# Dilated attention by residue class, with a joint softmax from exchanged maxima and sums

## What is computed

```python
for g, (window, dilation) in enumerate(DILATED_GROUPS):
    o_g, l_g = dilated_window_attention(q[:, :, g], k, v, window, dilation)
    outs.append(o_g)
    lses.append(l_g)
wts = jax.nn.softmax(jnp.stack(lses, axis=0), axis=0)
o = jnp.einsum('gbsh,gbshd->bshd', wts, jnp.stack(outs, axis=0))
y = o.reshape(Bsz, S, B_VW) * jax.nn.silu(z.astype(jnp.float32))
return y.astype(h.dtype) @ w_out
```

## Time and profile before

| what | us |
|---|---|
| median of 3 runs | 1556.77 |
| lowest and highest | 1555.94, 1557.71 |
| span of the profiled execution | 1553.7 |
| PE busy in the span | 1529.0 |
| DVE, ACT, POOL busy | 703.0, 601.9, 693.8 |

### The profile page before, as it was taken

How to read it: one execution, slowest core, us unless ns; L and a number is a source line. 1 busy time by engine, 2 the same in 40 slices (tenths; PEclk the granted TensorE clock), 3 DMA queues, 4 the chain that set the end, 5 groups by cost and what they waited for, 6 DMA issues and landing times.

```text
span 1553.7 us, 19713 instructions
## 1 busy us (share of the span) xinstructions
PE 1529.0 (98%) x7588; PEld 1253.4 (81%) x7588; DVE 703.0 (45%) x1147; ACT 601.9 (39%) x916; POOL 693.8 (45%) x312
## 2 busy tenths in 40 slices
PE   8999999999999999999999999999999999999898
PEld 7777967877888888888888888888888888887687
DVE  4258855482334226665654005630034346444733
ACT  6353254673332225122221115422444444355452
POOL 6423455334555535443434444444432435454532
PEclk9999999999999999999999999999999999999999
DMA  7314211102333332433332225543422322222021
GB/s 246 122 55 136 82 55 49 41 21 61 102 101 87 109 109 70 118 97 104 85 108 86 104 82 72 99 104 92 126 68 72 101 89 82 95 82 82 28 72 64
DMA packets 145126, 138.26 MB, mean 89 GB/s; under 512 B 7792, under 2 KB 118384, under 8 KB 145052
## 3 DMA queue, kind: packets, MB, share of 16 engines
q1 hardware_dynamic: 140836, 130.79, 29.3%
q10 hardware_dynamic: 4216, 6.45, 1.3%
HBM read 135.09 MB, written 2.13 MB: 88 GB/s over the span
## 4 chain that ended last, share of the span: by engine, by line
PE 90%; DVE 3%; ACT 3%; POOL 2%; issue 1%; DMA 0%; ACTq 0%; DVEq 0%; POOLq 0%
PE banks L732 87%; PE banks L761 2%; POOL w_lo L579 1%; PE banks L920 1%; PE banks L1350 0%; DVE prob L2552 0%; DVE xs L2072 0%; ACT w_hi L1474 0%; POOL prob L721 0%; DMA vec_rows<-in_norm_a 0%; ACT junk L1523 0%; ACT k L1938 0%; POOL prob L723 0%; ACT junk L1762 0%; DVE head_ms L2514 0%
## 5 line engine op out<-in xcount | busy, mean ns | idle before, releaser
L559 POOL TENSOR_TENSOR w_lo<-raw,w_hi 128x2048 fp32r<-128x2048 f32 x104 | 481.4, 4629 | 602.3 <-ACT w_hi L1474 602.3
L732 PE MATMUL banks<-h_hi,w_hi 128*128 128x512 f32 (+1 forms) x904 | 348.1, 385 | 2.4 <-DVE h_lo L2079 0.9
L732 PE MATMUL banks<-h_hi,w_lo 128*128 128x512 f32 (+1 forms) x904 | 340.4, 377 | 0.0
L732 PE MATMUL banks<-h_lo,w_hi 128*128 128x512 f32 (+1 forms) x904 | 340.1, 376 | 0.0
L1474 ACT ACTIVATE w_hi<-raw 128x2048 fp32r<-128x2048 f32 (+2 forms) x123 | 233.1, 1895 | 213.3 <-PE banks L732 203.1
L732 PEld LDWEIGHTS banks<-h_hi,w_hi 128*128 128x128 f32 x904 | 169.9, 188 | 42.1 <-issue 9.7
L732 PE MATMUL banks<-w_hi,h_hi 128*128 128x512 f32 (+1 forms) x544 | 199.8, 367 | 0.0
L732 PE MATMUL banks<-w_hi,h_lo 128*128 128x512 f32 (+1 forms) x544 | 198.2, 364 | 0.0
L732 PE MATMUL banks<-w_lo,h_hi 128*128 128x512 f32 (+1 forms) x544 | 198.1, 364 | 0.0
L732 PEld LDWEIGHTS banks<-h_hi,w_lo 128*128 128x128 f32 x904 | 169.6, 188 | 32.2
L732 PEld LDWEIGHTS banks<-h_lo,w_hi 128*128 128x128 f32 x904 | 169.9, 188 | 29.5
(11 more groups left out here) (319 smaller groups left out, 2348.6 us busy)
## 6 DMA issues: line engine op xcount, KB each, us to landing
raw<-in_w_in SPq DMA_DIRECT2D x56, 512.0 KB, 4.0
raw<-in_w_ffn_in SPq DMA_DIRECT2D x44, 512.0 KB, 5.0
...
```

The source lines that it names most:

```text
L559: pool.tensor_tensor(slot_of(w_lo, slot), slot_of(raw, slot), slot_of(w_hi, slot).bitcast(F32), ALU.subtract).then_inc(lo_made, 1)
L732: return pe.matmul(out, lhsT, rhs, start=start, stop=stop, **kw)
```

## The change

The groups with dilation 4 and 16 are computed by residue class. A query with row number 4j+c attends with dilation 4 to the rows 4i+c with i up to j, and with dilation 16 to those with j-i a multiple of 4. So for each head and each of the four residues c one tile of 128 queries by 128 keys holds everything, for both groups; window 512 and 2048 cut nothing off. There are 32 units now: 16 near ones (head, tile of 128 rows; 128 or 256 keys) and 16 far ones (head, residue; two tiles of 128x128 next to each other). Two units share a bank, and PE's order works in pairs of units.

What is needed for it: the copies of query groups 2 and 3 write `q3T` in the order of residues (ACT), POOL makes a copy `k3R` of the turned keys in this order (four copies of 128x512), and the values go to DRAM and come back as `v3R` (ACT's queue issues both). The near and the far units have different rows on their partitions, so for each pair of heads ACT sends the minima and sums of 16 units to DRAM and reads them back in the other order (`statistics_out`, `statistics_in`, four small transfers for a pair of heads); DVE makes the joint minimum (`gaps`), ACT the factors, DVE the shares (`shares`) with which it scales the exponents (`scaled_probs`). The turned far tiles are multiplied with `v3R` into every fourth column of the head's bank, on top of the near part.

The first slab of z3 is now done whole, the logits of the near units of heads 0 and 1 follow it, and the second slab is spread over the pairs 4 to 15. The gate silu(z) is no longer sigmoid times z: ACT takes exp(-z) (`exp_of_z3`), and DVE adds 1, takes the reciprocal and multiplies with z (`silu_of_z3`), each on 128x1024.

```diff
+    dist = p - np.arange(2 * P)[None, :] + P
+    back = p - f
+    dil = np.zeros((P, 4 * P), np.float32)
+    dil[:, 0:2 * P] = np.where((dist >= 0) & (dist <= 128), 0.0, NEG)
+    dil[:, 2 * P:3 * P] = np.where(back >= 0, 0.0, NEG)
+    dil[:, 3 * P:4 * P] = np.where((back >= 0) & (back % 4 == 0), 0.0, NEG)
...
+    k3R = place("k3_residues", 101.5, 4 * S)
+    v3R = arena("v3_residues", 56, NT * HALF)
+    near = [arena(f"near{h}", 72 + 3.5 * h, 7 * P) for h in range(4)]
+    far = [arena(f"far{a}", 86 + a, 2 * P) for a in range(4)]
+    far_sum = arena("far_sum", 64, 16 * P)
...
+        pool.wait_ge(rp_Tc, 4)
+        for h in range(4):
+            pool.tensor_copy(k3R[:, h * S:(h + 1) * S].rearrange("p (c j) -> p j c", c=4),
+                             k3T[:, h * S:(h + 1) * S].rearrange("p (j c) -> p j c", c=4)).then_inc(k_turned, 1)
...
+        for n in range(16):
+            u = 16 * (n // 8) + 8 + n % 8
+            buf = far[n % 4]
+            pool.wait_ge(dl_exp, u + 1)
+            pool.tensor_tensor(far_sum[:, n * P:(n + 1) * P], buf[:, 0:P], buf[:, P:2 * P], ALU.add).then_inc(dl_sum, 1)
+            if n in (1, 3, 5, 7):
+                lo_quarter(BASE["wout3"], n // 2)
+        for quarter in range(4):
+            lo_quarter(BASE["wout3"] + 1, quarter)
...
+        def z_steps(s, first, stop):
...
             g = BASE["z3"] + s
...
+            for n in range(first, stop):
+                b, k = divmod(n, KD)
+                ins = mm3(banks[:, 4 + 2 * s + b, :], hi[:, k, b * P:(b + 1) * P], lo[:, k, b * P:(b + 1) * P],
+                          h_hi[:, k * S:(k + 1) * S], h_lo[:, k * S:(k + 1) * S], k == 0, k == KD - 1)
+            if stop == 2 * KD:
+                ins.then_inc(slab_used, 1)
...
+        def pair_of_logits(pair):
+            bank = logit_bank(pair)
             for b in range(2):
...
+                x, far_unit, h, i = unit_of(2 * pair + b)
+                c0 = 256 * b
+                if far_unit:
+                    for w in (1, 2):
+                        ins = mm(banks[:, bank, c0 + (w - 1) * P:c0 + w * P], q3T[:, (4 * w + h) * S + i * P:(4 * w + h) * S + (i + 1) * P],
+                                 k3R[:, h * S + i * P:h * S + (i + 1) * P], True, True)
+                else:
+                    k0 = max(0, (i - 1) * P)
+                    ins = mm(banks[:, bank, c0:c0 + (i + 1) * P - k0], q3T[:, h * S + i * P:h * S + (i + 1) * P],
+                             k3T[:, h * S + k0:h * S + (i + 1) * P], True, True)
+            ins.then_inc(dl_log, 1)
...
+        for pair in range(4):
+            if pair < 2:
+                free(2 + pair)
+            else:
+                pe.wait_ge(dl_min, 2 * (pair - 2) + 2)
+            pair_of_logits(pair)
+        pe.wait_ge(ev_v, EV_V["q3"] + 12)
+        rope_transposes(3)
+        pe.wait_ge(lo_made, BASE["z3"] + 2)
+        pe.wait_ge(dl_min, 8)
+        z_steps(1, 0, 2)
         pe.wait_ge(rp_Tc, 16)
...
+        pe.wait_ge(k_turned, 4)
+        for pair in range(4, 16):
+            if pair >= 8:
+                pe.wait_ge(dl_min, 2 * (pair - 4) + 2)
+            pair_of_logits(pair)
+            n = pair - 4
+            z_steps(1, 2 + n + min(n, 2), 3 + n + min(n + 1, 2))
...
+        def turned(group):
...
+            pe.wait_ge(dp_norm, 8 * h + (2, 4, 8)[n])
...
+            bank = 4 + group % 2
+            if n < 2:
+                blocks = [near_at(h, t)[:, k:k + P] for t in (2 * n, 2 * n + 1) for k in range(0, 256 if t else P, P)]
+            else:
+                blocks = [far_sum[:, (4 * h + c) * P:(4 * h + c + 1) * P] for c in range(4)]
+            for m, block in enumerate(blocks):
+                ins = pe.transpose(banks[:, bank, m * P:(m + 1) * P], block, const("ident"))
+            ins.then_inc(dp_tr, 1)
...
+        def head_outputs(group):
...
+            out, probs = banks[:, 6 + h % 2, :], prob3T[group % 3]
+            pe.wait_ge(dp_copied, group + 1)
...
+                m = 0
+                for t in (2 * n, 2 * n + 1):
+                    for kt in range(max(0, t - 1), t + 1):
+                        ins = mm(out[:, t * P:(t + 1) * P], v3[:, kt * HALF + h * P:kt * HALF + (h + 1) * P], probs[:, m * P:(m + 1) * P],
...
+                if h == 0:
+                    pe.wait_ge(v_in, 16)
+                rows = out.rearrange("p (j c) -> p j c", c=4)
+                for c in range(4):
+                    ins = mm(rows[:, :, c], v3R[:, c * HALF + h * P:c * HALF + (h + 1) * P], probs[:, c * P:(c + 1) * P],
...
+        pe.wait_ge(ev_v, EV_V["z3"] + 1)
+        turned(0)
+        turned(1)
+        pe.wait_ge(ev_v, EV_V["z3"] + 2)
+        for group in range(2, 6):
+            head_outputs(group - 2)
+            turned(group)
+        head_outputs(4)
+        pe.wait_ge(dl_min, 32)
+        head_products(0, (0, 1))
+        head_outputs(5)
+        head_products(0, (2, 3))
+        head_products(1, (0, 1))
+        turned(6)
+        turned(7)
+        for group in range(8, 12):
+            head_outputs(group - 2)
+            turned(group)
+            if group == 8:
+                head_products(1, (2, 3))
+        head_outputs(10)
+        head_outputs(11)
         head_products(2, range(NT))
         head_products(3, range(NT)).then_inc(slab_used, 1)
...
+                src = banks[:, 4 * half + h, :]
+                if group >= 2:
+                    dst, src = dst.rearrange("p (c j) -> p j c", c=4), src.rearrange("p (j c) -> p j c", c=4)
...
+        def exp_of_z3(s):
...
+            act.activation(z3T[:, 2 * s * S:2 * (s + 1) * S], flat[:, 2048 + 1024 * s:3072 + 1024 * s], ACT.Exp, scale=-1.0).then_inc(ev_a, 1)
...
+        def exps_of(u):
...
+            act.activation(buf, buf, ACT.Exp, bias=stat_at(w_own, u, 0), scale=-1.0, accum_out=stat_at(w_own, u, 1)).then_inc(dl_exp, 1)
...
+        def statistics_out(x):
...
+            act.wait_ge(dl_exp, 16 * (x + 1))
+            act.dma_start(near_scratch[x].ap().rearrange("(t p) w -> p t w", p=P), w_own[x][:, 0:16].rearrange("p (t w) -> p t w", t=NT)).then_inc(st_out, 16)
+            act.dma_start(far_scratch[x].ap().rearrange("(j c) w -> j (c w)", c=4), w_own[x][:, 16:32]).then_inc(st_out, 16)
...
+        def statistics_in(x):
...
+            act.wait_ge(st_out, 32 * (x + 1))
...
+        act.wait_ge(v_out, 16)
+        act.dma_start(v3R[:], v_scratch.ap().rearrange("(j c) f -> j (c f)", c=4)).then_inc(v_in, 16)
+        for u in range(4):
+            exps_of(u)
+        rope_copies(3)
+        for u in range(4, 8):
+            exps_of(u)
+        exp_of_z3(0)
         split_hi(0, "z3", 1)
-        rope_copies(3)
...
+        for u in range(8, 16):
+            exps_of(u)
+        statistics_out(0)
+        for u in range(16, 32):
+            exps_of(u)
+            if u == 18:
+                statistics_in(0)
+            if u == 27:
+                factors(0)
+        statistics_out(1)
+        exp_of_z3(1)
+        split_hi(0, "wout3", 0)
+        for group in range(12):
+            copy_turned(group)
+            if group == 2:
+                statistics_in(1)
+            if group == 5:
+                factors(1)
         gated_addition("wout3", "g1", "pg1", "pp1", 8, None)
 
...
+        def silu_of_z3(s):
+            part = z3T[:, 2 * s * S:2 * (s + 1) * S]
             dve.wait_ge(ev_a, EV_A["z3"] + s + 1)
-            part = z3T[:, 2 * s * S:2 * (s + 1) * S]
+            link(dve.tensor_scalar(part, part, 1.0, None, ALU.add))
+            link(dve.reciprocal(part, part))
             dve.tensor_tensor(part, flat[:, 2048 + 1024 * s:3072 + 1024 * s], part, ALU.mult).then_inc(ev_v, 1)
...
+        def least(u):
...
+            x, far_unit, h, i = unit_of(u)
+            n = 2 * P if far_unit or i else P
+            dve.wait_ge(dl_log, u // 2 + 1)
+            if far_unit:
+                m = far_unit_no(u)
+                if m >= 4:
+                    dve.wait_ge(dl_sum, m - 3)
+                buf, mask = far[m % 4][:], dil[:, 2 * P:4 * P]
...
+            dve.tensor_tensor_reduce(out=buf, in0=banks[:, logit_bank(u // 2), c0:c0 + n], in1=mask, scale=-scale_c, scalar=3.0e38,
+                                     op0=ALU.add, op1=ALU.min, accum_out=stat_at(w_own, u, 0)).then_inc(dl_min, 1)
...
+        def gaps(x):
...
+            dve.wait_ge(st_in, 32 * (x + 1))
+            link(dve.tensor_tensor(pairs_of(w_joint[x][:]), of_kind(w_own[x], 0), of_kind(w_other[x], 0), ALU.min))
...
+        def shares(x):
...
+            link(dve.tensor_tensor(pairs_of(w_part[x][:]), pairs_of(w_factor[x][:, 16:32]), of_kind(w_other[x], 1), ALU.mult))
+            link(dve.tensor_tensor(w_part[x][:], w_part[x][:], w_joint[x][:], ALU.add))
+            link(dve.reciprocal(w_part[x][:], w_part[x][:]))
...
+        def scaled_probs(h):
...
+            for t in range(NT):
+                dve.tensor_scalar(near_at(h, t), near_at(h, t), share_at(h, 0, t), None, ALU.mult).then_inc(dp_norm, 1)
```

(24 more changed lines are left out.)

224 lines of the change are left out of this document (84 added, 140 removed).

## The result

| what | before | after |
|---|---|---|
| median, us | 1556.36 (4 runs) | 1570.47 (4 runs) |
| lowest and highest | 1555.61, 1557.71 | 1569.82, 1571.73 |
| span of the profiled execution | 1553.7 | 1568.9 |
| from the first z3 matmul to the second wout3 slab | 79.50 | 94.35 |

The changed kernel is slower: the ratio is 1.0092, with a 95% interval of 1.0080 to 1.0104. Nearly the whole difference of the spans, 15.2 us, lies in the stretch of which the prediction speaks (14.9 us); it runs from 1400.82 to 1495.17 in the trace after.

What follows compares the result with a forecast made beforehand. PE was taken to bound the kernel: 8.9 us of work saved, some 19.4 of waits added and 2.7 for the clock give +13.2 on the 1553.7 span, 1566.9; with 3.1 from span to median, 1570.0 us, range 1562 to 1577.

Steps and rivals of the forecast that it cites:

- PE's work saved: PE's work in the stretch falls from 70.8 to 61.9 us at full clock, saving 8.9 us.
- waits of PE, after less before: Longer PE waits in the stretch, mainly for DVE, ACT and the statistics, add some 19.4 us.
- slow clock: PE's clock falls after each of three long waits, up to 2.4 us each; 2.7 us counted in all.
- the weak step: Extending reciprocal times of one and four columns to 1024: 8.3 ns per column taken, 8.65 us each.
- the lower bound of 6 ns: A reciprocal slope of 6 ns per column would move the forecast from 1570.0 to 1565.3 us.
- Rival C: The reciprocal goes at an ordinary pace, each silu 3.1 us: 1552.4 us; chance 0.10 together with F.
- F: The silu is hidden in DVE's spare time, giving no more than C; chance 0.10 together with C.
- rival D: Strided operands are slow: far products' PSUM columns (+3.6 us) or ACT's copies (+3.2): 1571 to 1577; chance 0.15.
- rival E: The statistics' trip through DRAM lands in 7.8 us, +5 us on the forecast: 1575; chance 0.05.
- step 5: Statistics of heads 0 and 1 land in 2.5 us; PE idle 4.1 us ahead of turning group 0.
- Rival B: The clock stays up through PE's waits: +10.5 us, 1567.3 us; chance 0.20.
- five waits: PE idle 1.2 us ahead of transposes, 2.6 of pair 4, 6.9 of pair 12, 4.1 of turned groups, 11.2 of outputs.

Runs made afterwards that it cites:

- e9: e8 with the table loaded early and the exponents of units 8 to 15 ahead of gate and split; ratio to before 0.9937, median 1546.3 us.
- e1: The changed kernel without the two 128x1024 reciprocals, so the gate is computed differently; ratio to before 1.0014.
- e10: The changed kernel with the second silu done in two halves, head 0's outputs waiting for the first only; ratio to before 1.0080.
- e4: The changed kernel with exp(-z) of slab 0 ahead of ACT's last query scaling and the first silu behind unit 7's least value; ratio to before 1.0034.
- e3: The changed kernel with ACT's eight copies of q3T reading PSUM at every fourth column and writing contiguously; ratio to before 1.0057.
- e6: The changed kernel with far products written to 128 neighbouring columns instead of every fourth, misplacing that part of the result; ratio to before 1.0092.
- e2: The changed kernel with the gate of before, sigmoid on ACT and one multiplication on DVE, at the same places; ratio to before 1.0015.
- e8: The changed kernel with a tanh gate without reciprocal, contiguous copies ahead of the exponents, last gate in halves and other orders; ratio to before 0.9954.
- e5: The changed kernel with 34 unused 512-column matmuls on PE in its third wait, ahead of the outputs; ratio to before 1.0072.

## Why the prediction was right

The time was right within 0.5 us (1570.0 against 1570.47), the sign and the mechanism too: a reciprocal twice on PE's path. That it was right so closely is luck, because the errors of the sum cancel. By its own terms, in us (PE's work after is taken from e9, which has the same matmuls: 66.8 us busy, less 1.8, since its far products of head 0 and the next two groups take 3.7 us where full pace is 2.0, is 65.0):

| term | predicted | measured |
|---|---|---|
| PE's work saved | 8.9 | 73.9 - 65.0 = 8.9 |
| waits of PE, after less before | 19.4 | 21.3 - 5.6 = 15.7 |
| slow clock | 2.7 | 73.0 - 65.0 = 8.0 |
| sum | +13.2 | +14.8 |

The sum is 1.6 us short, and the step from the span to the median gives it back: I added 3.1 us, the median of several runs less the span of one, where each run on record is only 1.7 to 1.8 us longer than its own span (1570.61 and 1568.9 for the profiled one).

**PE's work.** The difference was right. Both sides were too small by 3 us: 70.8 for 73.9 and 61.9 for 65.0. A part of what I left out is in the rows of the changes of shape: the first 512-column matmul behind a pair takes 0.31 us to the next (1432.85 to 1433.16 in the changed kernel), the others 0.23.

**The reciprocal** was mis-sized: 6.55 us, not 8.65, 6.25 ns per column and not 8.3. The slope from one to four columns, 7.7, was the weak step that I named; the lower bound of 6 ns held it. The first silu took 9.4 us (its addition, beside POOL, 1.62 of them) and the second 8.5, not 10.6, and the two big waits were 4.3 and 8.6 us, not 6.9 and 11.2. The rest of the first difference is PE's: from the end of unit 15 it worked for 5.8 us more, not 4.5. e1 and e10 show that PE waits for the width of this instruction, e4 that it is its place which makes it wait. Rival C and F are out.

**ACT's strided copies** I took at nothing, with 3.2 us as the upper end. They take 0.94 us each in a row of four and not 0.50; PE's first two waits were 2.4 and 3.4 us instead of 1.2 and 2.6. e3 gives the worth: 5.4 us by the ratios, more than my upper end, since I had priced each copy and not what the longer waits do to the clock. This half of rival D was true, and I should have given it more than its share of 0.15. The other half, PSUM columns at a distance written by PE, cost nothing (e6).

**The statistics** landed in 1.8 to 3.6 us. These are the rows of the DMA issues in the stretch (KB each, median us to landing), which answer to the earlier trace rows:

```profile
near_scratch<-own ACTq DMA_DIRECT2D x2, 8.0 KB, 2.2
far_scratch<-own ACTq DMA_DIRECT2D x2, 8.0 KB, 3.6
other<-far_scratch ACTq DMA_DIRECT2D x2, 8.0 KB, 1.9
other<-near_scratch ACTq DMA_DIRECT2D x2, 8.0 KB, 1.8
```

My 2.5 was near, and rival E is out. The idle time of step 5 was 1.9 and not 4.1 us, because the statistics were there before PE had finished pair 15: DVE reads them at 1448.01, and PE works to 1454.7. What is left is DVE's way from pair 15's logits through two least values and the shares to the first scaling. It is 1.9 us in e1 and e2 as well, where the rows behind pair 12 have full pace, so it is not the clock that made it short. In e4 and e8 the statistics came last.

**The clock** was right in kind and too small by a factor of three. I let it fall three times and hid most of it behind DVE. It fell three times, but not at the same three: behind the waits that I had at 6.9 and 11.2 us (4.3 and 8.6), not behind the one that I had at 4.1 (1.9), and behind the one of 2.6 ahead of pair 4 (3.4), for which I had counted nothing. Each fall made PE's rows 2.6 to 2.9 us longer, a little more than my estimate of up to 2.4. Behind pair 4 and pair 12 the trace has DVE waiting for PE's logits, so that PE's slowness is not hidden there as I had it; no run tests these two falls by themselves, and where the first took the other course (e5, e6, e10), 1.8 us came back. No run shows the term of the sum, 4.7 us of work at half pace behind each wait and up to 2.4 us lost by it; in its place the changed kernel has windows of slow rows alone, at 0.50, of 6.0, 5.5 and 4.2 us, and 2.9, 2.7 and 2.6 us lost. The 4.7 us were my estimate from the program's start, where passes of 256 columns are 0.21 us apart at 12.57 and 0.12 at 13.85; but PE has already worked there from 4.03 us on, with pauses, and 4.7 us is only the last piece, from 8.88. The granted clock of the slow rows at the start reads 1.00, where the slow rows of the changed kernel read 0.50, so the start is not shown to be the same thing. Rival B is out, by the slow rows and by e5.

Of the five waits that I wrote down, their places and releasers were all right; only the sizes were off, by +1.2, +0.8, -2.6, -2.2 and -2.6 us.
